# State read and output products of the second block's mixers in 64x64 quarters of TensorE, with odd heads' outputs in the other token half

## The reference, cut to what matters

```python
def step(S, xs):
    u_n, w_n, qk_n, q_n, k_n, l_n = xs
    v_new = u_n - jnp.einsum('bhck,bhkv->bhcv', w_n, S)
    o_n = jnp.einsum('bhck,bhkv->bhcv', q_n, S) + jnp.einsum('bhij,bhjv->bhiv', qk_n, v_new)
    S = S * l_n[..., None, None] + jnp.einsum('bhck,bhcv->bhkv', k_n, v_new)
    return S, o_n
...
    o = rmsnorm_2(o, onorm_g) * jax.nn.silu(heads(z).astype(F32))
```

## Time and profile before

| | |
|---|---|
| median of three runs | 1558.51 us (1557.32 to 1558.82) |
| profiled execution, first to last instruction (the page gives no time around it) | 1558.8 us |
| mean granted TensorE clock | 0.995 |
| PE busy | 1525.1 us |
| DVE busy | 1188.6 us |
| ACT busy | 1017.6 us |
| the edited stretch in m0 | 748.28 to 768.09 us |
| the edited stretch in m1 | 1072.70 to 1092.50 us |

### The profile page before, as it was taken

How to read it: one execution, slowest core, us unless ns; L and a number is a source line. 1 busy time by engine, 2 the same in 40 slices (tenths; PEclk the granted TensorE clock), 3 DMA queues, 4 the chain that set the end, 5 groups by cost and what they waited for, 6 DMA issues and landing times.

```text
span 1558.8 us, 26842 instructions
## 1 busy us (share of the span) xinstructions
PE 1525.1 (98%) x9894; PEld 1308.5 (84%) x9894; DVE 1188.6 (76%) x1477; ACT 1017.6 (65%) x1431; POOL 60.4 (4%) x74
## 2 busy tenths in 40 slices
PE   7999999999999999999999999999999999999998
PEld 6988888878878888899888888998878888888886
DVE  5677877775578877787775556887688888888887
ACT  5667665566567656687465455875577777777775
POOL 0000000000000000020000000100000001101000
PEclk9999999999999999999999999999999999999999
DMA  7535455445424555464255555462699999999995
GB/s 269 195 119 189 167 211 188 177 147 189 169 102 165 213 188 184 142 190 144 80 192 187 204 181 184 162 167 83 227 373 368 394 387 381 369 396 385 364 362 210
DMA packets 54794, 351.08 MB, mean 225 GB/s; under 512 B 6208, under 2 KB 9968, under 8 KB 14896
## 3 DMA queue, kind: packets, MB, share of 16 engines
q1 hardware_dynamic: 46512, 330.94, 56.8%
q0 software_dynamic: 8192, 18.90, 4.7%
HBM read 341.90 MB, written 7.91 MB: 224 GB/s over the span
## 4 chain that ended last, share of the span: by engine, by line
PE 91%; DVE 4%; DMA 2%; ACT 2%; issue 1%; POOL 0%; SPq 0%; DVEq 0%; ACTq 0%
PE PS L917 20%; PE PS L1852 16%; PE PS L1985 14%; PE PS L2021 11%; PE PS L1870 8%; PE PS L1986 8%; PE PS L1478 1%; DVE EWL L3761 1%; PE PS L1083 1%; PE PS L1956 1%; DMA rows_m<-HN 1%; PE PS L1833 1%; DMA W<-in_weights 1%; PE PS L962 1%; PE PS L1547 1%
## 5 line engine op out<-in xcount | busy, mean ns | idle before, releaser
L3761 DVE TENSOR_TENSOR EWL<-W,EWH 128x2048 fp32r<-128x2048 f32 x144 | 329.6, 2291 | 45.4 <-ACT EWH L2789 45.2
L1985 PE MATMUL PS<-HTB,WH 128*128 128x512 f32 x944 | 329.3, 393 | 0.0
L2789 ACT ACTIVATE EWH<-W 128x2048 fp32r<-128x2048 f32 x144 | 276.5, 1920 | 61.3 <-PE PS L1870 34.2
L1986 PE MATMUL PS<-HTB,WL 128*128 128x256 f32 x1008 | 282.4, 280 | 0.0
L3087 DVE TENSOR_TENSOR WL<-W,WH 128x2048 fp32r<-128x2048 f32 x99 | 226.5, 2287 | 35.9 <-ACT WH L2216 32.8
L2216 ACT ACTIVATE WH<-W 128x2048 fp32r<-128x2048 f32 x99 | 189.2, 1918 | 95.4 <-PE PS L1986 84.6
L917 PE MATMUL PS<-MWH,HTB 128*128 128x256 f32 (+1 forms) x940 | 240.9, 341 | 2.1 <-issue 1.5
L3095 DVE TENSOR_TENSOR MWL<-W,MWH 128x1024 fp32r<-128x1024 f32 x136 | 164.5, 1220 | 85.2 <-ACT MWH L2240 83.2
L1985 PEld LDWEIGHTS PS<-HTB,WH 128*128 128x128 f32 x944 | 177.2, 188 | 40.1
L2240 ACT ACTIVATE MWH<-W 128x1024 fp32r<-128x1024 f32 x136 | 142.5, 1054 | 98.2 <-PE PS L917 89.8
L1986 PEld LDWEIGHTS PS<-HTB,WL 128*128 128x128 f32 x1008 | 189.5, 188 | 1.0
(11 more groups left out here) (413 smaller groups left out, 2441.1 us busy)
## 6 DMA issues: line engine op xcount, KB each, us to landing
W<-in_weights SPq DMA_DIRECT2D x311, 1024.0 KB, 4.9
CS<-in_consts POOLq DMA_DIRECT2D x4, 403.5 KB, 4.8
ARENA<-rows_m POOLq DMA_DIRECT2D x8, 192.0 KB, 6.2
ARENA<-rows_m POOLq DMA_DIRECT2D x2, 768.0 KB, 12.2
moe_acc<-X POOLq DMA_DIRECT2D x3, 512.0 KB, 12.1
moe_rows<-HN POOLq DMA_DIRECT2D x3, 512.0 KB, 12.1
X<-in_x SPq DMA_DIRECT2D x2, 512.0 KB, 4.4
W<-in_weights SPq DMA_DIRECT2D x2, 512.0 KB, 7.1
```

The source lines that it names most:

```text
L1985: mm(PS[b][:, :], WH[:, sl, o:o + P], HTB[:, :, kk, :], start=(kk == 0), stop=False, skip_group_check=True)
L1986: ins = mm(PS[b][:, 0:256], WL[:, sl, o:o + P], HTH[:, kk, :], start=False, stop=(kk == KC - 1), skip_group_check=True)
L2789: A(EWH[tile % SPLIT][:, :], tile_ap(w0 + tile), ACT.Copy).then_inc(sem("moe_hi"), 1)
L3761: TT(EWL[tile % SPLIT][:, :], tile_ap(w0 + tile), EWH[tile % SPLIT][:, :].bitcast(F32), SUB).then_inc(sem("moe_lo"), 1)
```

## The change

The zeros beside the heads' states go. `S` becomes 128x64 per column group (head 2c in the lower partitions, 2c+1 in the upper), and each head is read by itself in a 64x64 product. `state_read` is merged into `state_out`: for each column group and each half r it issues one query product and one key product, in four different quarters of the array. The quarter's output half is `n % 2 ^ r`, so the outputs of odd heads land in the partitions of the other chunk. `chunk_read` adds to these, so it too writes odd heads into the other half; it is split into even heads (r = 0) and odd heads (r = 1), and the second part waits for the first by a semaphore. On DVE `new_values` and `gated` read even and odd heads apart, `state` works on 128x192, and the memset is gone. The wait for the scaled queries `_qd` moves ahead of `state_out(1)`.

```diff
-    m2.S = a(768).rearrange("p (b c v) -> p b c v", b=2, c=3)
+    m2.S = a(384).rearrange("p (b c v) -> p b c v", b=2, c=3)
+    a(384)
...
             def state_out(n):
 
-                key, t = (m, "vp", n), n // 2
+                key, out = (m, "vp", n), (m, "o", n // 2)
                 cols = slice(n * CH, (n + 1) * CH)
                 claim(pe, key)
+                if n in (1, 2):
+                    claim(pe, out)
                 await_free_of(pe, (m, "kv", n - 1))
                 await_free_of(pe, (m, "w", n % 2))
                 for c in range(3):
-                    ins = mm(bank(key)[half[n % 2], c * P:(c + 1) * P], m2.WT[:, c, cols], m2.S[:, n % 2, c, :], start=True, stop=True)
+                    for r in range(2):
+                        h, o = 2 * c + r, 2 * c + 1 - r
+                        mm(bank(out)[half[n % 2 ^ r], h * 64:(h + 1) * 64], m2.QD[half[r], c, cols], m2.S[half[r], n % 2, c, :],
+                           start=(c == 0 and n < 3), stop=False, skip_group_check=True)
+                        ins = mm(bank(key)[half[n % 2 ^ r], o * 64:(o + 1) * 64], m2.WT[half[1 - r], c, cols], m2.S[half[1 - r], n % 2, c, :],
+                                 start=True, stop=True)
                 done(ins, key)
...
-            def chunk_read(t):
+            def chunk_read(t, r):
 
                 key = (m, "o", t)
-                for h in range(6):
+                if r:
+                    pe.wait_ge(sem(m + "_even_read"), t + 1)
+                for h in range(r, 6, 2):
                     for c in range(2):
-                        ins = mm(bank(key)[half[c], h * 64:(h + 1) * 64], m2.ATQ[half[c], t, h, :], m2.UU[half[c], t, h * 64:(h + 1) * 64],
+                        ins = mm(bank(key)[half[c ^ r], h * 64:(h + 1) * 64], m2.ATQ[half[c], t, h, :], m2.UU[half[c], t, h * 64:(h + 1) * 64],
...
-            chunk_read(0)
+            chunk_read(0, 0)
             fx_scores(2)
+            chunk_read(0, 1)
...
-            chunk_read(1)
+            chunk_read(1, 0)
             for n in range(NT):
                 await_free_of(pe, (m + "f", "o", n))
             for j in range(2):
                 transposed(m, j, M2_OT[j])
+            chunk_read(1, 1)
...
                 if n:
-                    link(TT(S1, m2.S[:, n % 2], m2.EGB[:, :, e:e + 1].broadcast_to([P, 3, P]), MUL))
...
+                    link(TT(S1, m2.S[:, n % 2], m2.EGB[:, :, e:e + 1].broadcast_to([P, 3, CH]), MUL))
                 await_full(dve, key)
-                for r in range(2):
-                    p = slice(64 * r, 64 * r + 64)
-                    s1, new = S1[p, :, p], bank(key)[p, 0:192].rearrange("p (g v) -> p g v", g=3)
-                    ins = TT(s1, s1, new, ADD) if n else dve.tensor_copy(s1, new)
-                release(ins, key)
+                new = v3(bank(key)[:, 0:192], 3)
+                release(TT(S1, S1, new, ADD) if n else dve.tensor_copy(S1, new), key)
...
-                release(TT(m2.UU[rp, t, :], m2.UU[rp, t, :], bank(key)[rp, 0:384], SUB), key)
+                uu = h3(m2.UU[:, t, :])
+                for r in range(2):
+                    at = slice(64 * (1 - n % 2 ^ r), 64 * (1 - n % 2 ^ r) + 64)
+                    ins = TT(uu[rp, r::2, :], uu[rp, r::2, :], h3(bank(key)[at, 0:384])[:, r::2, :], SUB)
+                release(ins, key)
...
-                link(TT(h3(dst), h3(bank(key)[:, 0:384]), bc(st_or[:, t * 8:t * 8 + 6], 2, 64), MUL))
+                src, root = h3(bank(key)[:, 0:384]), st_or[:, t * 8:t * 8 + 6]
+                TT(h3(dst)[:, 0::2, :], src[:, 0::2, :], bc(root[:, 0::2], 2, 64), MUL)
+                for c in range(2):
+                    here, there = slice(64 * c, 64 * c + 64), slice(64 - 64 * c, 128 - 64 * c)
+                    ins = TT(h3(dst)[here, 1::2, :], src[there, 1::2, :], bc(root[there, 1::2], 2, 64), MUL)
+                link(ins)
...
-            dve.memset(m2.S, 0.0).then_inc(sem(m + "_s0"), 1)
```

More of the change, by code:

```diff
@@ L1631, in state_out @@
                 for c in range(3):
-                    ins = mm(bank(key)[half[n % 2], c * P:(c + 1) * P], m2.WT[:, c, cols], m2.S[:, n % 2, c, :], start=True, stop=True)
-                done(ins, key)
[L1635 to L1643, removed]
-            def chunk_read(t):
+                    for r in range(2):
[4 more added lines that the diff above has]
+                                 start=True, stop=True)
+                done(ins, key)
+            def chunk_read(t, r):
                 key = (m, "o", t)
-                for h in range(6):
+                if r:
+                    pe.wait_ge(sem(m + "_even_read"), t + 1)
+                for h in range(r, 6, 2):
                     for c in range(2):
-                        ins = mm(bank(key)[half[c], h * 64:(h + 1) * 64], m2.ATQ[half[c], t, h, :], m2.UU[half[c], t, h * 64:(h + 1) * 64],
-                                 start=(t == 0 and c == 0 and h == 0), stop=(h == 5), skip_group_check=True)
-                done(ins, key)
+                        ins = mm(bank(key)[half[c ^ r], h * 64:(h + 1) * 64], m2.ATQ[half[c], t, h, :], m2.UU[half[c], t, h * 64:(h + 1) * 64],
+                                 start=False, stop=True, skip_group_check=True)
+                if r:
+                    done(ins, key)
+                else:
+                    ins.then_inc(sem(m + "_even_read"), 1)
             def m2_chunk(c, **flags):
@@ L1691, in mixer2 @@
             fx_turn(0)
+            pe.wait_ge(sem(m + "_qd"), 1)
             state_out(1)
@@ L1694, in mixer2 @@
             pool_projected()
-            pe.wait_ge(sem(m + "_qd"), 1)
-            state_read(1)
             state_in(1)
@@ L1706, in mixer2 @@
             state_out(2)
-            state_read(2)
             fx_values(1)
@@ L1711, in mixer2 @@
             state_out(3)
-            state_read(3)
             fx_values(2)
             await_free_of(pe, (m, "vp", 3))
-            chunk_read(1)
+            chunk_read(1, 0)
             for n in range(NT):
@@ L3569, in state @@
                 if n:
-                    link(TT(S1, m2.S[:, n % 2], m2.EGB[:, :, e:e + 1].broadcast_to([P, 3, P]), MUL))
-                else:
-                    dve.wait_ge(sem(m + "_s0"), 1)
+                    link(TT(S1, m2.S[:, n % 2], m2.EGB[:, :, e:e + 1].broadcast_to([P, 3, CH]), MUL))
                 await_full(dve, key)
-                for r in range(2):
-                    p = slice(64 * r, 64 * r + 64)
-                    s1, new = S1[p, :, p], bank(key)[p, 0:192].rearrange("p (g v) -> p g v", g=3)
-                    ins = TT(s1, s1, new, ADD) if n else dve.tensor_copy(s1, new)
-                release(ins, key)
+                new = v3(bank(key)[:, 0:192], 3)
+                release(TT(S1, S1, new, ADD) if n else dve.tensor_copy(S1, new), key)
                 await_free_of(dve, key)
```

## The result

| | before | changed |
|---|---|---|
| median (21 runs each) | 1558.82 us | 1561.24 us |
| lowest and highest | 1557.32 to 1559.59 | 1559.17 to 1565.93 |
| ratio | | 1.0018 (95%: 1.0012 to 1.0024) |
| profiled execution, first to last instruction | 1558.8 us | 1559.1 us |

A forecast was written before the change was run, and what follows sets the result against it. PE, 98% busy, and DVE were taken as two almost full lists handing work to each other. Each mixer's output matrix starts 0.27 us sooner; 2 x 0.27 = 0.5 off the median 1558.5 gives 1558.0 us, range 1555.6 to 1560.4.

The forecast's parts named there:

- Steps 1 to 5: m0, from `state(0)` to the turn of `attn_out`'s output: each hand-over comes sooner, the turn by 0.77 us.
- the bank of head 3's scores: At `fx_scores(2)` PE must wait until DVE empties this bank; DVE takes back 0.4 us of PE's 1.45.
- the run of `gated(0)`, `new_values(3)` and `attn_out`: DVE sequence late in the stretch, with 0.2 us of slack or less, growing by 0.65 us.
- Step 6: Behind the turned output: odd heads' products take 0.50 us there, so the output matrix starts 0.27 us sooner.
- of 5.4 us that PE's list loses, 4.9 turn into waits for DVE: Both mixers: most of PE's saved work becomes waiting for DVE, leaving 0.5 us off the span.
- its signs: Expected profile: `state_out` 0.50 us, PE waiting at `fx_scores(2)`, for `new_values(3)` (about 0.5) and the attention output (0.8).
- The two rivals: PE alone sets the end, 1553.1 us, chance 0.13; the quarters don't run together, 1562.2 us, chance 0.07.
- PE alone: Rival: PE's saving in both mixers is won in full, 5.4 us, giving 1553.1 us; chance 0.13.
- The quarters ran together: Merged `state_out`: passes overlap at 14.4 ns; the rival denied this, 1.54 us a group, 1562.2 us, chance 0.07.
- 29 ns: Upper-end price of a pass in merged `state_out`: group 0.85 us, +0.6 us a mixer, 0.3 slower than before.
- 58: Rival's price in ns of a `state_out` pass if passes into one bank from both row halves come in turn; chance 0.07.
- The lower bound: Per mixer: free changes of form and DVE pairs at 0.31 us, -0.5; with memset's 0.6, about -1.2: 1556.1 us.

The follow-up runs named there:

- the filled waits: Changed kernel with useless turns of the identity put ahead of PE's four waits in each mixer: 1559.50 us, 1.0007 against the kernel before.
- the products near: Changed kernel with the odd heads' `chunk_read` products right behind the even heads': 1558.02 us, 0.9994 against the kernel before.
- two more moves: Changed kernel, `gated(0)` behind `attn_out`, plus odd heads' products right behind even ones and head 5's softmax ahead of `new_values(2)`: 1554.17 us, 0.9969 against before.

## Why the prediction was wrong

The local steps held. All times here are counted from the start of head 0's turn, in m0.

| step | forecast | measured |
|---|---|---|
| merged `state_out`, to the next group | 0.50 | 0.51 |
| `fx_scores(2)` starts | 4.41 | 4.49 |
| `fx_values(0)` starts | 5.77 | 5.87 |
| `new_values(2)` starts | 8.52 | 8.66 |
| `gated(0)` starts | 12.03 | 12.26 |
| `new_values(3)` starts | 13.88 | 14.16 |
| turn of the attention's output | 15.97 | 16.26 |
| output matrix | 17.08 | 17.57 |

Steps 1 to 5, the bank of head 3's scores and the run of `gated(0)`, `new_values(3)` and `attn_out` came as worked out, each hand-over a little later than taken, 0.29 us in all. **Step 6 failed by a missing term**: behind the turned output I counted 0.50 for the odd heads' products, but the turn is now followed by another form too, and takes 0.81 (764.12 to 764.93) instead of 0.61 (767.46 to 768.07). Both together make the stretch 0.22 us longer and not 0.27 shorter, 1.0 us over both mixers. That by itself would have left the kernel at about 1559.3, inside the range.

**What broke the range is a step that I did not have**: "of 5.4 us that PE's list loses, 4.9 turn into waits for DVE". I priced these waits as time that is merely not won. In the runs they have a price of their own: in a third of the executions or more a mixer falls to 1.2 GHz, for 3.4 to 10.2 us in the traces, and the longest fall lost 3.0 us in its mixer (25.95 against 22.92). On the median that is 0.9 to 1.5 us by the filled waits, and 1.6 by the runs at 0.996 (1561.24 against 1559.66); without it the kernel had stayed inside the range. I had read that the clock was 1.00 in both stretches, and took it as given after the change. One wait was missing from the list as well: for head 5's exponent, 0.6 us, which the prediction neither counts nor names among its signs. In both traces with a fall of 10.2 us the clock fell within 0.2 us of the end of this wait (at 1084.29 in the changed kernel, at 1084.98 with the products near). The Trainium skill describes such an event ("TensorE: Matmul & The Clock Gate", HAM oscillation — how this bites in real kernels): in its example waits for DMA of about 3 to 5 us between short bursts of matmuls throttle the engine again. The trace agrees that waits bring the clock down, but here waits of 0.6 to 0.8 us were enough, which that example would not lead one to expect; the measurement decides. I had drawn on the page for the packing of small products alone.

The two rivals were rightly put low. PE alone did not set the end. The quarters ran together at 13 to 14 ns a pass, so 29 ns or 58 were too high. Neighbours in one row half cost nothing: the group takes 0.51 us and not 0.85, so the rule of the Trainium skill ("TensorE: Matmul & The Clock Gate", The mechanism) that weights load beside a running product only when the row group differs does not hold for this pattern. Both banks were filled from both row halves without a loss, each half writing its own partitions of the bank, so the rule of the Trainium skill on one bank ("TensorEngine Tiling (Array Packing)", Gotcha 1: PSUM Pressure), read that broadly, does not hold here either.

The profile itself misled in one point: I set its span beside the median as if both were the same quantity, while 1.8 us lie around a span, and the profiled execution had been slow ahead of the stretch. It cost nothing, since the sum was made of distances. The lower bound was summed too high: 0.27, 0.5 and 0.6 us a mixer give 1555.8 and not 1556.1, which the range held all the same.

What stays open: why a fall comes in one execution and not in the next, with the same waits. The runs give frequencies and no rule for it. Nor is it known where the clock fell in the runs without a trace. That the steady part of the loss is DVE's split instructions was not tried by undoing these alone; their durations are in the trace.

## What to carry to other kernels

When an edit takes work from TensorE in a stretch where it hands work to and fro with other engines, list who is late next and count the new waits; each is a risk for the clock and not just time not won, so look at the spread of the runs and the clock of each, not at one profile, and look in the trace where the clock was low, since a mean over the whole run mixes in stretches that have nothing to do with the edit. Then move work that nobody waits for (here the gated output) behind the step that TensorE waits for: that turned +1.8 us against the kernel before into -2.5 in the same set of runs, and with two more moves it became -4.4. If nothing can be moved, useless products in the waits can be cheaper than the falls, as they were here.

## What the runs showed of the hardware

- Waits of 0.6 us, with TensorE busy in between, were enough to bring its clock from 2.4 to 1.2 GHz in some executions. Counted by a mean clock at or below 0.994, it was 12 of 32 runs of the changed kernel, 0 of 78 of the one before, 0 of 11 with the waits filled, 5 of 5 with one of them 1.1 to 1.4 us longer.
- The stretches at 1.2 GHz in the mixers were 3.4, 6.8 or 10.2 us long. Those behind the edited code, which every trace of both kernels has, were 6.8 or 10.2 us.
- A change of the array's form cost 0.15 to 0.2 us at the borders worked out here (behind small passes, and behind the turned output), as much as 11 to 14 small passes in four quarters.
- 64x64 passes over four quarters started every 13 to 14 ns, also where neighbouring products share a row half (24 passes within 0.31 us).
